# Decode keys copied to scratch while V is projected, scored by head pair in phases 0 to 5; softmax in the last projection, most values in the second norm

## What is computed

```python
k_past = cache_k[page_table].reshape(db, -1, FA_HEADS, FA_HEAD_DIM)      # 8 x 512 x 16 x 64, 32 pages
v_past = cache_v[page_table].reshape(db, -1, FA_HEADS, FA_HEAD_DIM)
logf_past = cache_logf[page_table].reshape(db, -1, FA_HEADS)
# forget_attend, for the one new token of each sequence
logits = jnp.einsum('nqhd,nkhd->nhqk', q, k) * (FA_HEAD_DIM ** -0.5)
decay = c_q[..., :, None] - c_k[..., None, :]                            # c: cumulative sum of logf
p = jax.nn.softmax(jnp.where(causal, logits + decay, -jnp.inf), axis=-1)
o = jnp.einsum('nhqk,nkhd->nqhd', p, v)
y = (o * jax.nn.silu(z)) @ w_out + b_out
x = layer_norm(DEEPNORM_ALPHA * x + (1.0 + gate) * y, ln_g[layer], ln_b[layer])
```

## Time and profile before

| | us |
|---|---|
| median of 3 runs | 1778.09 |
| lowest, highest | 1773.65, 1780.67 |
| the profiled execution | 1777.73 |
| its span, first to last instruction | 1776.3 |

### The profile page before, as it was taken

How to read it: one execution, slowest core, us unless ns; L and a number is a source line. 1 busy time by engine, 2 the same in 40 slices (tenths; PEclk the granted TensorE clock), 3 DMA queues, 4 the chain that set the end, 5 groups by cost and what they waited for, 6 DMA issues and landing times.

```text
span 1776.3 us, 27940 instructions
## 1 busy us (share of the span) xinstructions
PE 1656.2 (93%) x10096; PEld 1434.5 (81%) x10096; DVE 1010.4 (57%) x1568; ACT 623.9 (35%) x980; POOL 419.0 (24%) x432
## 2 busy tenths in 40 slices
PE   6999989999999988999889999999999999867976
PEld 4899989999999988999767777777777877655742
DVE  3433254334333347225567676767768686899875
ACT  2212122111121226225443645545464636451121
POOL 0000011011011010002132434425162524444221
PEclk8999999999999998999999999999999999988986
DMA  8111112212222212224323112221212121338667
GB/s 359 36 48 35 47 60 96 83 63 91 83 78 75 84 59 87 96 100 149 95 86 116 60 60 60 71 71 59 82 36 83 56 74 36 99 120 303 223 248 298
DMA packets 50191, 180.45 MB, mean 102 GB/s; under 512 B 6522, under 2 KB 8186, under 8 KB 48850
## 3 DMA queue, kind: packets, MB, share of 16 engines
q1 hardware_dynamic: 31650, 116.11, 19.3%
q0 software_dynamic: 18480, 63.53, 9.9%
HBM read 154.07 MB, written 17.15 MB: 96 GB/s over the span
## 4 chain that ended last, share of the span: by engine, by line
PE 75%; DVE 11%; issue 5%; ACT 3%; DMA 3%; POOL 2%; POOLq 1%; SPq 0%; DVEq 0%; ACTq 0%
PE bank L1684 19%; PE bank L1686 18%; PE bank L1685 18%; PE bank L2046 2%; PE bank L2000 2%; PE bank L2048 2%; PE bank L2047 2%; PE bank L1819 2%; PE bank L2028 1%; PE bank L2027 1%; DVE bank L1384 1%; DMA fsw<-units 1%; POOL p_lo L533 1%; PE bank L1799 1%; PE bank L1903 1%
## 5 line engine op out<-in xcount | busy, mean ns | idle before, releaser
L1684 PE MATMUL bank<-h_hi,w_lo 128*128 128x344 f32 x1152 | 374.5, 325 | 9.9 <-DVE h_lo L1076 8.7
L1685 PE MATMUL bank<-h_lo,w_hi 128*128 128x344 f32 x1152 | 369.0, 320 | 0.0
L1686 PE MATMUL bank<-h_hi,w_hi 128*128 128x344 f32 x1152 | 368.7, 320 | 0.0
L533 POOL TENSOR_TENSOR p_lo<-parg,p_hi 128x512 fp32r<-128x512 f32 (+1 forms) x192 | 214.0, 1132 | 173.0 <-ACT p_hi L919 172.5
L1684 PEld LDWEIGHTS bank<-h_hi,w_lo 128*128 128x128 f32 x1152 | 217.6, 189 | 14.8 <-issue 12.3
L1684 PE MATMUL bank<-x_hi,w_lo 128*128 128x512 f32 x528 | 220.8, 418 | 6.6 <-POOL x_lo L485 6.5
L1685 PEld LDWEIGHTS bank<-h_lo,w_hi 128*128 128x128 f32 x1152 | 217.8, 189 | 0.2 <-issue 0.2
L1686 PEld LDWEIGHTS bank<-h_hi,w_hi 128*128 128x128 f32 x1152 | 217.6, 189 | 0.0
L1686 PE MATMUL bank<-x_hi,w_hi 128*128 128x512 f32 x528 | 208.8, 395 | 0.0
L1685 PE MATMUL bank<-x_lo,w_hi 128*128 128x512 f32 x528 | 208.7, 395 | 0.0
L1684 PE MATMUL bank<-y_hi,w_lo 128*128 128x320 f32 (+2 forms) x512 | 180.6, 353 | 29.6 <-DVE w_lo L1034 19.0
(11 more groups left out here) (301 smaller groups left out, 2644.5 us busy)
## 6 DMA issues: line engine op xcount, KB each, us to landing
raw<-units SPq DMA_DIRECT2D x121, 512.0 KB, 3.4
ada_ring<-w_ada SPq DMA_DIRECT2D x32, 512.0 KB, 3.3
pages<-cache_k POOLq DMA_DIRECT2D x32, 512.0 KB, 5.0
pages<-cache_v POOLq DMA_DIRECT2D x32, 512.0 KB, 7.8
ada_first<-w_ada SPq DMA_DIRECT2D x8, 1024.0 KB, 14.9
ckb<-scr_c POOLq DMA_DIRECT2D x16, 512.0 KB, 4.5
KX<-KA SPq DMA_DIRECT2D x32, 256.0 KB, 4.3
xT<-x_t SPq DMA_DIRECT2D x2, 2064.0 KB, 23.3
```

The lines of the kernel that those rows point to most:

```text
L533: g.tensor_tensor(p_lo[:, r, off:HALF], parg[:, r, off:HALF], p_hi[:, r, off:HALF].bitcast(F32), ALU.subtract).then_inc(S("p_ready"), 1)
L1684: mm(out, lhs_lo, rhs_hi, start=first, stop=False)
L1685: mm(out, lhs_hi, rhs_lo, start=False, stop=False)
L1686: return mm(out, lhs_hi, rhs_hi, start=False, stop=last)
```

## The change

- **Copy.** While V of the gMLP is projected, POOL copies the 32 key pages from the cache to `scr_k` and the log-forget pages to `scr_f`, both in HBM, in the order of the table.
- **Scores by pair.** In phases 0 to 5 DVE scores one head pair (128 of the 1024 features) for all 32 pages in four steps of eight pages: `score_mul(j, c)` and `score_sum(j, c)`, on one buffer `kpb` of 512 KB. SP loads it from `scr_k` (`load_keys`), stores the query of the next phase to `scr_q` straight from `kqvzS` (`put_q`), loads it back broadcast (`get_q`), and stores the scores of a phase to `scr_s` (`put_scores`).
- **The last two pairs.** Their keys (`kp2`, two loads of 2 MB) come in phase 7, and `score_late` scores them in eight steps behind the phases, in the first three blocks of the last projection. `gather_scores` brings all into `scol`.
- **Phase 7.** The turn of the queries, its copy, three scores and all page loads are gone from it.
- **Softmax and values.** The turns stand behind halves 2 and 3 of the last projection, the transposes and logits behind half 6, the weights behind half 8, and the first two value steps behind halves 11 and 12. The other six stand in the second norm, two more of them ahead of the last two transposes.
- **Loads and the tail.** The first four value sets are loaded in the last projection. `fsw` is loaded by SP instead of POOL, when the last `r2T` is there. The decode output's mask, gate, projection and norm are put between the norms of the last tiles.

```diff
+            pool.wait_ge(S("lo_ready"), 4)
+            for b in range(NS):
+                for p in range(NP):
+                    page = pool.value_load(ptab[0:1, b * NP + p:b * NP + p + 1], min_val=0, max_val=cache_k.shape[0] - 1)
+                    pool.dma_start(scr_k[b * NP + p, :, :], cache_k[bass.ds(page, 1), :, :].rearrange("a t f -> (a t) f"))\
+                        .then_inc(S("pages_in0"), 16)
...
+            def put_q(j):
+
+                sp.wait_ge(S("ev_s"), 4 * j + 2)
+                settle(sp, S("settled"))
+                sp.dma_start(scr_q[bass.ds(j, 1), :, :].rearrange("a n p -> p (a n)"), kqvzS[:, 1, j, 0:NS], allow_slow_non_contiguous=True).then_inc(S("scr_q"), 16)
...
+            def load_keys(j, c):
+
+                wait(sp, S("pages_used"), 4 * j + c)
+                settle(sp, S("settled"))
+                sp.dma_start(kpb[:, :, :, :].rearrange("p b a f -> p (b a) f"),
+                             scr_k[2 * NP * c:2 * NP * (c + 1), :, bass.ds(j * P, P)].rearrange("n t f -> t n f")).then_inc(S("kp_in"), 16)
+
+            def load_phase(j, scored):
+                load_swapped(j)
+                load_b(j + 1, 0)
+                load_b(j + 1, 1)
+                load_keys(j, 1)
+                load_b(j + 1, 2)
+                load_keys(j, 2)
+                load_keys(j, 3)
+                load_b(j + 1, 3)
...
+            def score_mul(j, c):
+
+                dve.wait_ge(S("kp_in"), 16 * (4 * j + c + 1))
+                if c == 0:
+                    dve.wait_ge(S("qb_in"), 16 * j + 16)
+                settle(dve, S("settled"))
+                v.tensor_tensor(kpb[:, :, :, :], kpb[:, :, :, :], by_key(qb, c), ALU.mult).then_inc(S("qk_prod"), 1)
...
-            for b in range(NS):
-                if b < 2:
-                    pool.wait_ge(S("pages_used"), NS - 1 + b)
-                elif b == 2:
-                    pool.wait_ge(S("fa_mm"), 2 * KB)
-                elif b >= 4:
-                    pool.wait_ge(S("pages_used"), NS + b - 3)
-                load_values(b, b % 4)
...
+            for n in range(NS):
+                if n < 2:
+                    pool.wait_ge(S("pages_used"), SCORED - 4 + 4 * n)
+                elif n < 4:
+                    pool.wait_ge(S("pages_used"), SCORED + n - 1)
+                elif n == 4:
+                    pool.wait_ge(S("fa_mm"), 2 * KB)
+                elif n >= 6:
+                    pool.wait_ge(S("pages_used"), SCORED + n - 3)
+                load_values(n)
...
+            ln_forward(0, r2T, TT)
+            ln_forward(1, r2T, TT)
+            for n in range(2, 6):
+                decode_values(n)
+                ln_forward(n, r2T, TT)
+            decode_values(6)
+            decode_values(7)
```

More of the change, by code:

```diff
@@ L404, in _ @@
             for q in range(4):
                 load_b(0, q)
[L406 to L409, removed]
+            sp.wait_ge(S("ln1_back"), TT)
+            load_query(0)
+            sp.wait_ge(S("pages_in0"), MOVED)
+            load_keys(0, 0)
+            load_phase(0, True)
+            with sp.Fori(1, LATE - 1) as j:
+                load_phase(j, True)
+            load_phase(LATE - 1, False)
@@ L410, in _ @@
+            load_swapped(LATE)
+            for q in range(4):
+                load_b(LATE + 1, q)
+            put_q(KB - 1)
+            load_swapped(KB - 1)
             sp.wait_ge(S("mm"), 12 * KB - 5)
@@ L577, in _, with load_values @@
                             pattern=[[1, NS], [0, H]], channel_multiplier=-1).then_inc(S("pc"), 1)
[L579 to L592, removed]
+            def load_values(n):
+                s, (odd, p) = VALUE_SLOT[n], divmod(n, NP)
                 for g in range(4):
@@ L1376, in peak, with gather_scores @@
+            def gather_scores():
+                dve.wait_ge(S("late_in"), 48)
+                dve.wait_ge(S("pages_used"), SCORED)
+                for p in range(NP):
+                    last = v.tensor_copy(scol[:, p, :, :].rearrange("q b (j h) -> q b j h", h=2),
+                                         sct[:, :, :, p, :].rearrange("q j b h -> q b j h"))
+                last.then_inc(S("sn_ready"), 1)
             def peak(j, qt):
@@ L1486, in _, with phase @@
             kq_low(0, 0)
-            def phase(j, more):
+            def phase(j, more, keys):
                 later = not isinstance(j, int) or j > 0
@@ L1546, in phase @@
                     split_lo(j + 1, 2)
-                else:
-                    score(0)
                 exponents(j, 9)
+                if keys:
+                    score_mul(j, 3)
+                exponents(j, 10)
+                if keys:
+                    score_sum(j, 3)
                 if not more:
-                    score(1)
-                exponents(j, 10)
-                if not more:
-                    score(2)
                     y2_low(0)
@@ new lines, in _ @@
+                    if n == 3:
+                        tok(3, vtok, 2)
+                        score_late(5)
+                    if n == 4:
+                        new_key()
+                        score_late(6)
+                    if n == 5:
+                        score_late(7)
+                        gather_scores()
+                    if n == 6:
+                        decay()
+                        logits()
+                    if n == 7:
+                        weights()
+                    if n == 8:
+                        spread_weights()
@@ L2119, in phase @@
                 values(j, 2)
-                if not more:
-                    pe.wait_ge(S("zs_done"), 4 * KB)
-                    turn(1, 0)
                 steps(37, 38)
@@ L2231, in _ @@
                 last.then_inc(S("fs_used"), 1)
+            ln_forward(7, r2T, TT)
             for h in range(2):
```

420 lines of the change are left out of this document (244 added, 176 removed).

## The result

The changed kernel takes 1765.0 us (median; 1762.02 to 1768.78), where the kernel before takes 1778.09; the ratio is 0.9938, 95% interval 0.9924 to 0.9953. Forecast were 1755 us, with a range of 1740 to 1778, and a gain of 23 us; the gain is 11 us by the ratio and 13 by the medians. The profiled execution has a span of 1763.4 us instead of 1776.3, so 12.9 us are to be found in the two traces.

The account below looks back on a forecast made before the run. TensorE was taken to bound the phases, decode attention on VectorE and the DMA queues the tail from 1592 us on. Terms +4 - 8 - 13 - 6 = -23 on 1777.73 gave 1755 us, range 1740 to 1778.

Parts of the forecast that it names:

- Copy in the V stage: V stage: GpSimd's issue of the key copies is hidden and weight loads have 21.8 us of cover; 0 us.
- Scores in phases 0 to 5: Phases 0 to 5: VectorE's multiplies and GpSimd's subtractions exclude each other, stalling TensorE 0.7 us a phase; +4 us, ends 0 and +22.
- p_lo on the path: Phases 0 to 5: three multiplies a phase and p_lo block each other, 22 us in place of 4; 1773 us, chance 0.14.
- late keys: Phases 0 to 5: third and fourth multiply wait for keys landing late; at 14 us landing 67 us, 1818 us, chance 0.08.
- the step on the query's store: Phases: transposed store in 4 B pieces has some 20 us before the next phase's first multiply; 0 up to that.
- The last phase: Phase 7: without the query turn, its copy and three scores, fa_first starts earlier; -8 us, ends -5 and -10.
- The last projection: Last projection: 97.6 us instead of 110.5, with the 10.17 us wait for the third weight gone; -13 us, ends -8 and -17.
- The end: Behind the projection: 66.6 us instead of 72.2, last value set at +38.4, then 26.3 us of VectorE work; -6 us.
- the 358 of the Trainium skill: The end: HBM to SBUF transfers bound near 358 GB/s, 14.1 MB take 39.4 us; gain 2 us instead of 6.
- The rival in which GpSimd's queue is served first: The end: value sets land at +25, fsw last at +38; 57.5 us in place of 66.6, 1746 us, chance 0.12.

Follow-up runs that it names:

- the run with small scores: Changed kernel with VectorE's score multiplies and reductions of phases 0 to 5 cut to 8 and 16 values a partition, loads and waits kept; 1763.51 us (0.9928).

## Why the prediction was right or wrong

**Copy in the V stage (0): right.** The mark behind it moved by 0.2 us.

**Scores in phases 0 to 5 (+4): the size was below, and the price was paid elsewhere.** The marks give +1.1 us, the run with small scores 1.0. Multiplies and p_lo do get in each other's way, as the term has it, but it is the subtractions that grow, by 15 us in the six phases, while a multiply takes 1289 ns on average and 1.56 us at most. The stall of TensorE behind them, which the term priced at 0.7 us a phase, did not come: its waits for p_lo stayed at 3.2 us. What the 1.0 us is made of isn't shown. The keys landed in 4.2 us in the middle, close to the 4.1 of the earlier trace rows, and no multiply waited for them. Both rivals that hang on this, p_lo on the path and late keys, fell.

**What failed is the step on the query's store.** It says: "The query's transposed store in pieces of 4 B has no row; its chain has some 20 us before the first multiply of the next phase, so it is 0 up to that." That asks only who waits for the store. It lands in 8 to 10.5 us in every phase, in time for its own reader, as said. But in front of phase 0 it runs beside `f_out` and `scr_c`, and TensorE waits for what follows them; and the "next phase" argument doesn't hold for the first one, whose query and keys are loaded just ahead of KX and `ckb`. The prediction looks at SyncE's queue inside the loop and doesn't follow it at its first turn. It put at nothing what measured 11.7 us. Large pieces for this store alone give back 9.8 to 11.7 of them; with the small pieces kept, the loads moved behind `ckb` give back 6.7. Without this loss the sum would have been 24.7 us of gain, near the 23 forecast. That 1765.0 still lies inside the range of 1740 to 1778 is no merit of the working: the range was wide enough for a loss that none of its rivals names.

**The last phase (-8): right,** -7.5 with the 0.5 of phase 6 beside it. The 4.41 us wait for p_lo and the turn's 1.91 us are gone. Late next is the wait on rc at 1559.51, 3.82 us instead of 2.58.

**The last projection (-13): right, a little more came, -15.4.** 95.1 us instead of 110.5 and of 97.6 forecast. The sum held 2 us of waits, and there were none from 1601 to 1692.

**The end (-6): the direction held, and half of the size.** 69.5 us instead of 66.6. The last value set landed and was used at +39.7, not at +38.4, and its matmuls take 3.26 us ahead of the mask where the sum has 1.9, so the mask starts at +43.0, not +40.3. Behind it the sum has 26.3 us (its own terms add up to 26.5), and it measured 26.5. The rate was as taken from the earlier trace rows: from 1697 to 1733 us the mean was 404 GB/s, and the 358 of the Trainium skill, which would have given a gain of 2, isn't borne out by this rate (though the gain came out near 2, for another reason). The rival in which GpSimd's queue is served first fell in the trace and in the run that put `fsw` behind two sets: the queues share.

The sum of what came: 0.2 + 11.8 + 1.1 - 0.5 - 7.5 - 15.4 - 2.7 = -13.0 us.

## What to carry to other kernels

A DMA that is moved or added has two prices: who waits for it, and what stands beside it and behind it on its way; look up for both, and at the first turn of a loop apart from the others. Count pieces as well as bytes: a transposed store of 4 KB in 1024 pieces held up its neighbours for 4 to 7 us. (The runs compare 1024 pieces of 4 B with 128 of 32 B, and don't separate the number from the size.) And where two queues carry data for the end of a program, issuing one ahead of the other isn't enough: here it paid to hold the less urgent one back until all but the last set of the other had landed.

## What the runs showed of the hardware that I had not expected

- A store of 4 KB from 128 partitions to HBM takes 1.5 us in pieces of 32 B and 8 to 11 in pieces of 4 B, and in that time stores of 64 KB from another queue land in 6 to 9.5 us instead of 2.2 to 2.3.
- A VectorE multiply of 128x1024 whose second SBUF input has a stride of 8 values takes 2.26 us instead of 1.29 on average.
- Where such multiplies and GpSimd's subtractions meet, GpSimd's grow: 15 us in six phases, against 1.6 us of all 24 multiplies over 1.22 each.
- The last page of 512 KB on GpSimd's queue took 16.7 us to land when 4 MB were issued on SyncE's queue around it, and 12.5 when these were issued 5.6 us behind it.
